# Two products in place of three for an expert's second tile of 64 rows

## The reference

```python
def moe_swiglu(h, router, wg, wu, wd):
    t = h.reshape(B * S, D)
    logits = (t @ router).astype(jnp.float32)
    top_v, top_i = lax.top_k(logits, TOP_K)        # 2 of 8 experts
    gates = jax.nn.softmax(top_v, axis=-1)
    ...
    for e in range(N_EXPERTS):
        out = out + comb[:, e:e + 1] * swiglu(t, wg[e], wu[e], wd[e])
```

## Time and profile before

| | us |
|---|---|
| runs: median (three runs) | 1533.51 |
| runs: lowest, highest | 1531.31, 1538.21 |
| profiled execution: span, first to last instruction | 1534.7 |
| expert stage, 952.67 to 1495.20 of it | 542.5 |

### The profile page before, as it was taken

One profiled execution on the slowest core, in us unless ns is written; L12 is line 12 of the kernel. 1 busy time (PEld: TensorE's weight loads), 2 busy tenths in 40 slices (PEclk: granted clock), 3 DMA queues, 4 the chain that ended last, 5 costly groups with the idle time before them and its releaser, 6 DMA issues.

```text
span 1534.7 us, 16496 instructions
## 1 busy us (share of the span) xinstructions
PE 1350.8 (88%) x6063; PEld 1077.7 (70%) x6063; DVE 954.3 (62%) x1241; ACT 660.3 (43%) x816; POOL 126.5 (8%) x147
## 2 busy tenths in 40 slices
PE   2998989799999999979889962999999999999990
PEld 2775447688887888767744741898988987787770
DVE  5956862756465455664665063455565578888885
ACT  4435432522222221343455131445444467676763
POOL 1260050000000000023000002000000000000004
PEclk9999989899999999989999975999999999999995
DMA  9931331165547354535400008656556579999964
GB/s 345 303 110 55 124 123 58 39 205 176 167 144 238 112 204 153 199 104 178 171 0 1 0 0 316 229 180 228 188 183 236 195 284 353 349 386 352 352 259 178
DMA packets 141810, 286.93 MB, mean 187 GB/s; under 512 B 6926, under 2 KB 48444, under 8 KB 141756
## 3 DMA queue, kind: packets, MB, share of 16 engines
q1 hardware_dynamic: 131116, 250.29, 47.1%
q0 software_dynamic: 10496, 35.92, 6.4%
q10 hardware_dynamic: 144, 0.00, 0.0%
HBM read 265.74 MB, written 20.45 MB: 186 GB/s over the span
## 4 chain that ended last, share of the span: by engine, by line
PE 77%; DVE 11%; ACT 4%; issue 4%; DMA 2%; POOL 1%; SPq 0%; ACTq 0%; POOLq 0%; DVEq 0%
PE ps L553 21%; PE ps L555 21%; PE ps L554 21%; PE ps L565 3%; DVE acc L1327 3%; PE ps L715 2%; ACT spl L1206 2%; PE ps L734 2%; PE ps L694 2%; DVE spl L1716 1%; DVE xfull L1725 1%; PE ps L703 1%; DMA x<-in_x 1%; DVE tmpm L1365 1%; DVE x L1369 1%
## 5 line engine op out<-in xcount | busy, mean ns | idle before, releaser
L1716 DVE TENSOR_TENSOR spl<-mraw,spl 128x2048 fp32r<-128x2048 f32 (+1 forms) x146 | 308.5, 2116 | 155.4 <-ACT spl L1206 154.5
L1206 ACT ACTIVATE spl<-mraw 128x2048 fp32r<-128x2048 f32 (+1 forms) x146 | 258.2, 1775 | 202.6 <-PE ps L555 171.9
L553 PE MATMUL ps<-spl,xgT 128*128 128x512 f32 (+1 forms) x528 | 199.1, 377 | 9.8 <-DVE xgT L1729 6.3
L1012 ACT ACTIVATE spl<-raw 128x2048 fp32r<-128x2048 f32 (+2 forms) x56 | 100.7, 1799 | 232.9 <-PE ps L555 193.7
L555 PE MATMUL ps<-spl,xgT 128*128 128x512 f32 (+1 forms) x528 | 197.1, 373 | 0.0
L554 PE MATMUL ps<-spl,xgT 128*128 128x512 f32 (+1 forms) x528 | 196.8, 373 | 0.0
L553 PE MATMUL ps<-hT,spl 128*128 128x512 f32 x416 | 165.2, 397 | 7.9 <-DVE hT L1388 7.9
L1311 DVE TENSOR_TENSOR spl<-raw,spl 128x2048 fp32r<-128x2048 f32 (+2 forms) x56 | 120.9, 2158 | 75.1 <-ACT spl L1012 74.5
L555 PE MATMUL ps<-hT,spl 128*128 128x512 f32 x416 | 163.8, 394 | 0.0
L554 PE MATMUL ps<-hT,spl 128*128 128x512 f32 x416 | 163.7, 393 | 0.0
L1327 DVE SCALAR_TENSOR_TENSOR acc<-raw,cond,acc 128x512 f32<-128x512 f32 x154 | 118.7, 771 | 5.4
(11 more groups left out here) (290 smaller groups left out, 2092.2 us busy)
## 6 DMA issues: line engine op xcount, KB each, us to landing
raw<-in_w_mod SPq DMA_DIRECT2D x48, 1024.0 KB, 6.2
mraw<-in_moe_w_down SPq DMA_DIRECT2D x40, 1024.0 KB, 6.4
mraw<-in_moe_w_gate SPq DMA_DIRECT2D x34, 1024.0 KB, 5.4
mraw<-in_moe_w_up SPq DMA_DIRECT2D x32, 1024.0 KB, 6.5
mraw<-in_moe_w_gate SPq DMA_DIRECT2D x16, 768.0 KB, 6.7
mraw<-in_moe_w_up SPq DMA_DIRECT2D x16, 768.0 KB, 6.8
raw<-in_ffn_w_gate SPq DMA_DIRECT2D x11, 1024.0 KB, 8.1
raw<-in_ffn_w_up SPq DMA_DIRECT2D x11, 1024.0 KB, 5.4
```

Of the source, the lines that this page charges most:

```text
L553: mm(o, lh, rh, start=start, stop=False)
L1012: A(spl[:, s % SPLS, 0, 0:n], raw[:, r % RAWS, 0:n], ACT.Copy).then_inc(hi_ready, 1)
L1206: A(spl[:, (SB + j) % SPLS, 0, 0:w], mraw[:, j % MRAWS, 0:w], ACT.Copy).then_inc(hi_ready, 1)
L1716: V.tensor_tensor(o[:, 1, 0:w], mraw[:, j % MRAWS, 0:w], o[:, 0, 0:w].bitcast(F32), ALU.subtract).then_inc(lo_ready, 1)
```

## The change

The second tile of a two-tile pass has 64 rows in place of 128, so such a pass serves 192 rows; the slots, the loads of rows and the stores follow. An expert with 129 to 192 rows takes one pass of two tiles; with 193 to 256 it would take that and one of one tile more.

The half tile is kept as one operand of 128 columns, its 64 high parts beside its 64 low parts (xhT, ahT). Two products serve it, this operand against the weights' high and against their low part (mm2). In PSUM partitions 0 to 63 then hold the products of the high parts, 64 to 127 those of the low parts, and the two halves must be added. For gate and up ScalarE copies the lower half to partitions 0 to 63 and VectorE adds the upper; for the output too. SiLU of the half tile reads the sum. The product low x low, which mm3 leaves out, is in it.

```diff
-MAXI, MAX2 = 12, 7
+MAXI, MAX2 = 13, 7
+HP = P // 2
+MORE_THAN = (0, P, P + HP, 2 * P + HP, 3 * P)
+ROWS2 = P + HP
...
-        xgT = [at(f"xgT{b}", HT_ + 16384 + 8192 * b, [P, 2, KD, P], F32R) for b in range(2)]
+        xgT = at("xgT0", HT_ + 16384, [P, 2, KD, P], F32R)
+        xhT = at("xhT", HT_ + 16384 + 8192, [P, KD, 2, HP], F32R)
...
-        aT = [at(f"aT{b}", W_ + 31232 + 11264 * b, [P, 2, NB, P], F32R) for b in range(2)]
+        aT = at("aT0", W_ + 31232, [P, 2, NB, P], F32R)
+        ahT = at("ahT", W_ + 42496, [P, NB, 2, HP], F32R)
...
+                next_row = first_row + (ROWS2 if tiles == 2 else P)
                 for b in range(tiles):
                     eng.wait_ge(xg_ps[b], i + 1)
-                    g.dma_start(xg[b][:], tiles_dram[bass.ds(first_row + P * (tiles + b), P), :]).then_inc(xg_dma[b], 16)
+                    g.dma_start(xg[b][0:height(b), :], tiles_dram[bass.ds(next_row + P * b, height(b)), :]).then_inc(
+                        xg_dma[b], 16)
...
-                eng.wait_ge(xg_dma[b], count * 16)
                 for k in range(KD):
-                    last = tr(ps[:, 2 * b + k // 4, P * (k % 4):P * (k % 4) + P], xg[b][:, P * k:P * k + P])
+                    if b:
+                        last = nc.tensor.transpose(ps[:, 2, HP * k:HP * k + HP], xg[1][0:HP, P * k:P * k + P],
+                                                   ident[0:HP, 0:HP])
+                    else:
+                        last = tr(ps[:, k // 4, P * (k % 4):P * (k % 4) + P], xg[0][:, P * k:P * k + P])
                 last.then_inc(xg_ps[b], 1)
 
+            def mm2(o, both, weight, start, stop):
+
+                wh, wl = weight
+                mm(o, both, wh, start=start, stop=False)
+                return mm(o, both, wl, start=False, stop=stop)
+
             def item(i, tiles):
+
+                def product(b, o, whole, half, k, weight, start, stop):
+
+                    if b:
+                        return mm2(o, half[:, k].rearrange("p h q -> p (h q)"), weight, start, stop)
+                    return mm3(o, hi_lo(whole, k, 0, P), weight, start, stop)
...
                     for b in range(tiles):
                         eng.wait_ge(e_mul[b], i * 3 + (c + 1))
+                    for b in range(tiles):
                         for q in range(EW[c][1] // P):
-                            last = tr(ps[:, bank + 2 * b, P * q:P * q + P], acte[b][:, P * q:P * q + P])
+                            if b:
+                                last = nc.tensor.transpose(ps[:, bank + 2, HP * q:HP * q + HP],
+                                                           acte[1][0:HP, P * q:P * q + P], ident[0:HP, 0:HP])
+                            else:
+                                last = tr(ps[:, bank, P * q:P * q + P], acte[0][:, P * q:P * q + P])
                         last.then_inc(aT_ps[b], 1)
...
-                                    last = mm3(ps[:, 2 * b + part, 0:w], hi_lo(xgT[b], k, 0, P), u(kk, 0, w),
-                                               k == 0, k == KD - 1)
+                                    last = product(b, ps[:, 2 * b + part, 0:w], xgT, xhT, k, u(kk, 0, w),
+                                                   k == 0, k == KD - 1)
...
+                        A(sge[0][:, 0:w], ps[:, 0, 0:w], ACT.Silu).then_inc(e_silu[0], 1)
+                        if tiles == 2:
                             if c:
-                                eng.wait_ge(e_mul[b], i * 3 + c)
-                            A(sge[b][:, 0:w], ps[:, 2 * b, 0:w], ACT.Silu).then_inc(e_silu[b], 1)
+                                eng.wait_ge(e_mul[1], i * 3 + c)
+                            A(sge[1][0:HP, 0:w], ps[HP:P, 2, 0:w], ACT.Copy).then_inc(gate_low, 1)
+
+                    def silu_half(c):
+
+                        eng.wait_ge(gate_sum, i * 3 + (c + 1))
+                        w = EW[c][1]
+                        A(sge[1][0:HP, 0:w], sge[1][0:HP, 0:w], ACT.Silu).then_inc(e_silu[1], 1)
+
+                    def up_half(c):
+
+                        eng.wait_ge(w_used, i * EU + (SB + 4 * c + 4))
+                        w = EW[c][1]
+                        A(acte[1][0:HP, 0:w], ps[HP:P, 3, 0:w], ACT.Copy).then_inc(up_low, 1)
...
+                        if tiles == 2 and j in (5, 9, 13):
+                            silu_half(j // 4 - 1)
+                        if tiles == 2 and j in (6, 10, 14):
+                            up_half(j // 4 - 1)
...
+                    A(ye[0][:].rearrange("p (h c) -> p h c", h=2), ps[:, 4:6, :], ACT.Copy).then_inc(ye_ev[0], 1)
+                    if tiles == 2:
+                        A(ye[1][0:HP, :].rearrange("p (h c) -> p h c", h=2), ps[HP:P, 6:8, :],
+                          ACT.Copy).then_inc(ye_low, 1)
...
-                for r in range(T):
-                    ins = V.tensor_scalar(above[:, r, :], cnt[:], float(P * r), None, ALU.is_gt)
+                for r, rows_before in enumerate(MORE_THAN):
+                    ins = V.tensor_scalar(above[:, r, :], cnt[:], float(rows_before), None, ALU.is_gt)
                 link(ins)
                 V.tensor_tensor(pairs[:, 1], above[:, 0], above[:, 2], ALU.add)
                 link(V.tensor_tensor(pairs[:, 0], above[:, 1], above[:, 3], ALU.add))
+                link(V.tensor_tensor(pairs[:, 1], pairs[:, 1], above[:, 4], ALU.add))
...
+                        src = ps[:, 2, HP * k:HP * k + HP] if b else ps[:, k // 4, P * (k % 4):P * (k % 4) + P]
+                        ins = V.tensor_scalar(xfull[:, k, 0:height(b)], src, modn[:, 3, k:k + 1], modn[:, 2, k:k + 1],
+                                              ALU.mult, ALU.add)
                     ins.then_inc(xg_full[b], 1)
                     eng.wait_ge(xg_hi[b], count)
-                    V.tensor_tensor(xgT[b][:, 1], xfull[:], xgT[b][:, 0].bitcast(F32), ALU.subtract).then_inc(
-                        xg_ready[b], 1)
+                    if b:
+                        V.tensor_tensor(xhT[:, :, 1, :], xfull[:, :, 0:HP], xhT[:, :, 0, :].bitcast(F32),
+                                        ALU.subtract).then_inc(xg_ready[1], 1)
+                    else:
+                        V.tensor_tensor(xgT[:, 1], xfull[:], xgT[:, 0].bitcast(F32), ALU.subtract).then_inc(
+                            xg_ready[0], 1)
...
+                    def gate_half(c):
+
+                        w = EW[c][1]
+                        eng.wait_ge(gate_low, i * 3 + (c + 1))
+                        V.tensor_tensor(sge[1][0:HP, 0:w], ps[0:HP, 2, 0:w], sge[1][0:HP, 0:w], ALU.add).then_inc(
+                            gate_sum, 1)
+
+                    def multiply_half(c):
+
+                        w = EW[c][1]
+                        o = acte[1][0:HP, 0:w]
+                        eng.wait_ge(up_low, i * 3 + (c + 1))
+                        V.tensor_tensor(o, ps[0:HP, 3, 0:w], o, ALU.add).then_inc(up_sum, 1)
+                        eng.wait_ge(up_sum, i * 3 + (c + 1))
+                        eng.wait_ge(e_silu[1], i * 3 + (c + 1))
+                        V.tensor_tensor(o, sge[1][0:HP, 0:w], o, ALU.mult).then_inc(e_mul[1], 1)
...
                     for j in range(2, EU + 2):
                         if j in (6, 10, 14):
                             multiply((j - 6) // 4)
+                        if tiles == 2 and j in (7, 11, 15):
+                            multiply_half((j - 7) // 4)
                         part(i, j)
+                        if tiles == 2 and j in (4, 8, 12):
+                            gate_half(j // 4 - 1)
...
+                    if tiles == 2:
+                        eng.wait_ge(ye_low, i + 1)
+                        o = ye[1][0:HP, :].rearrange("p (h c) -> p h c", h=2)
+                        V.tensor_tensor(o, ps[0:HP, 6:8, :], o, ALU.add).then_inc(ye_ev[1], 1)
```

More of the change, by code:

```diff
@@ L189, in build @@
         cnt = little("cnt", [P, E])
-        above = little("above", [P, T, E])
+        above = little("above", [P, len(MORE_THAN), E])
         pairs = little("pairs", [P, 2, E])
@@ L318, in xn_of, with height @@
             return xnf if s == 2 else xn
+        def height(b):
+            return HP if b else P
         def unit_size(j):
@@ L532, in _ @@
             with eng.Fori(0, n2) as i:
-                item(i, 2, i * (2 * P))
+                item(i, 2, i * ROWS2)
             with eng.Fori(n2, n) as i:
-                item(i, 1, (i + n2) * P)
+                item(i, 1, i * P + n2 * HP)
             for t in range(T):
@@ L940, in item @@
                             for h in range(2):
-                                last = mm3(ps[:, 4 + 2 * b + h, :], hi_lo(aT[b], f0 + q, 0, P), u(q, 512 * h, 512),
-                                           f0 + q == 0, f0 + q == NB - 1)
+                                last = product(b, ps[:, 4 + 2 * b + h, :], aT, ahT, f0 + q, u(q, 512 * h, 512),
+                                               f0 + q == 0, f0 + q == NB - 1)
                     last.then_inc(w_used, 1)
@@ L948, in item @@
```

(49 more changed lines are left out.)

28 lines of the change are left out of this document (18 added, 10 removed).

## The result

The changed kernel takes 1494.35 us (median of four runs, 1490.87 to 1497.01) against 1532.57 us. The ratio is 0.9733, 95% interval 0.9714 to 0.9752, which is 40.9 us less (38.0 to 43.8); the two medians alone lie 38.2 us apart. Timed again later it was 0.9740 (0.9713 to 0.9767). Forecast were 1490 us and 43.5 us less. The measured time is inside the range, with the gain 2.6 us too large by the ratio and 5.3 by the medians. The span of its profiled execution is 1495.2 us.

A forecast was written before the change was run, and what follows sets the result against it. TensorE was taken as the only bound of two-tile passes. Three passes at -14.1 us (-42.3) plus start and routing (-1.2) gave -43.5 us, from 1533.5 to 1490.0 us; range 1483 to 1498.

The forecast's parts named there:

- products: In each two-tile pass, the second tile's 70 sets go from three products to two at an unchanged beat: -15.0 us.
- transposes: The second tile's 19 transposes per two-tile pass move 64 columns in place of 128; width hardly counts: -0.1 us a pass.
- wait at the third turn: At the third turning of activations, TensorE waits for VectorE's half-tile add and multiply behind a subtraction: +1.0 us a pass.
- wait at the end of a pass: Before the next pass's first unit, VectorE's subtraction still comes in time, 0.9 us to spare: no wait.
- start: At the expert stage's start, the second tile's first rows come earlier, removing a TensorE wait: -1.5 us.
- routing: One more compare and one more linked add on the way to the scatter: +0.3 us.
- rival (a): The forecast itself for the whole kernel: 1484 to 1495 us, cuts of 49.2 to 38.7 us; chance 0.81.
- Rival (d): TensorE's beat in the new products is shorter because two in a row share their stationary operand: under 1484 us; chance 0.03.

The follow-up runs named there:

- the narrow kernel: Against the changed kernel, the half tile unpacked: three products from 64-column operands, adds and copies taken out; ratio 1.0017 to the kernel before.
- the kernel with separate waits: Against the changed kernel, TensorE at the stage's start turns the first tile's rows before waiting for the second's; cast to second tile's first product 37.24 us.

## Why the prediction was right, and where it was off

The mechanism was right where it counted, in the products and in the wait; the sum was 2.5 us too large, by terms, for three passes:

| term | forecast | measured |
|---|---|---|
| products | -45.0 | -44.7 (14.9 a pass) |
| transposes | -0.3 | +1.2 (4.22 against 3.82 us a pass) |
| wait at the third turn | +3.0 | +3.2 |
| wait at the end of a pass | 0 | 0 |
| start | -1.5 | -0.9 |
| routing | +0.3 | +0.3 |

The measured terms add up to -40.9, beside the 41.0 from the copy to the end. All misses went the same way, so none hid another. The time, 1494.35, is near the upper end of rival (a), 1495.

**Products.** Right: the beat stayed at 0.2267 us, for both members of a pair, and a pass lost 70. That it is the count of products and not the rows is shown by the narrow kernel. Rival (d) is out.

**Transposes.** The term that was mis-sized most. I held that the moving width hardly counts and that half of it would cost no more, from products with one column and the full 128 partitions. The narrow transposes read 64 partitions and move 64 columns. The turns of activations became 0.12, 0.13 and 0.20 us dearer, and the turn of the rows 0.05 cheaper. The Trainium skill's page "TensorE: Matmul & The Clock Gate", section "Back-to-back issue gap", gave, as an estimate, a gain of 0.6 us a pass from the width, and its section "LDWEIGHTS (loading the stationary operand)" none; neither says that it could cost. The starts in the timelines narrow down why it does. Three, four or eight wide ones ahead of a narrow one take 0.45, 0.53 and 0.97 us until it starts, 0.13 to 0.16 more than half of the all-wide turn took before (0.29, 0.40, 0.83). The narrow ones behind them, until the next product, take 0.33, 0.38 and 0.64: (0.64 - 0.38) / 4 = 0.065 us each, an estimate, where a wide one takes 0.10. So a narrow transpose by itself looks cheaper, and a fixed cost where the shape changes is more than three or four of them give back. No run tests this reading, for instance by narrow ones alone, and whether the width or the 64 partitions make them cheaper stays open.

**The third turn.** Forecast 1.0 us, measured 1.05, removed by moving one multiplication and lengthened by adding to it.

**End of a pass.** No wait, but 0.3 us to spare and not 0.9. All three row ops shrank, by 1.5 us together, but the subtraction for the next pass's first unit waits for ScalarE both before and after (0.39 us in rows 8, 0.58 with the change). What brings it forward is what stands ahead of ScalarE's splits, the scalings and ScalarE's own copy, 0.97 us: counted from the turn of the rows it came 0.95 earlier. VectorE's smaller subtraction (0.54 us) is not on that path, and I had counted it in.

**Start.** 1.62 us of wait fell to 0.2, and from the first tile's first product to the second's it took 5.61 us in place of 7.10: the 1.5 us that were forecast. But the first tile's first product came 0.6 us later after the cast, 32.13 in place of 31.55. I had followed the second tile alone and missed that the waits for both loads now stand ahead of the first tile's transposes, though I had named just that for the activations. By the kernel with separate waits 0.36 us of this is that wait's doing.

The median was 4.3 us above the forecast, more than these 2.5. The measured ratio applied to the median that the forecast started from, 1533.5, gives 1492.6; the rest is that medians of a few runs scatter by a us or two, since executions differ by some us ahead of the stage.

## To carry to other kernels

A pass that TensorE fills from end to end was shortened here by taking products away, and not by fewer stationary columns or shorter weight loads. When such a pass gets faster, look for the one place where the fewest products stand between a producer's signal and its use, since that is where VectorE's work, done in the order written, first showed, and put the short op that is waited for ahead of the long one that isn't. Packing that relies on the data (192 rows) should be set against its price on the other side, here a whole pass of 51 us.

## What the runs showed of the hardware that was not expected

- A stationary operand of 64 columns is loaded in 134 ns in place of 188, yet products with it follow each other at 0.230 us, with 128 columns at 0.2267.
- Four transposes of 128x128 and four of 64 partitions and 64 columns took 0.91 us together, eight of 128x128 took 0.79; with eight and eight it was 1.61 us against 1.66 for sixteen wide ones.
- A wait of 1.83 us on a busy TensorE was followed by a stretch at the clock of 1.2 GHz in one of three passes; waits of 0.9 us in the same place were not, in any of the 18 passes that had one.
- With the same program up to there, executions reach the routing between 911.7 and 920.2 us, and this goes with the mean granted clock from 100 to 300 us: 0.91 in the seven that reach it from 915.9 on, 0.93 in the two at 913.9, and 0.94 in the three at 911.7 to 912.5.
